# Sixteen gate projections as two-by-two block products, on one core of a Trainium2 chip

## The reference

```python
proj = jnp.einsum('bsd,de->bse', x, w_in[l])            # 1024 x 1024 times 1024 x 5120
ya = _stick_breaking_attention(qa, ka, va)              # 8 heads of 64
yb = _rms_norm(_differential_attention(q1, q2, k1, k2, vb, lam), subln_gain[l])   # 4 heads
gate_a = jax.nn.sigmoid(proj[..., c_vb:c_ga])           # 1024 x 1024
gate_b = jax.nn.sigmoid(proj[..., c_ga:])               # 1024 x 1024
merged = gate_a * einsum(ya, w_branch_a) + gate_b * einsum(yb, w_branch_b)
x = _layer_norm(ALPHA * x + einsum(merged, w_out), ln1_gain, ln1_bias)
h = jnp.square(jax.nn.relu(einsum(x, w_ff1)))
x = _layer_norm(ALPHA * x + einsum(h, w_ff2), ln2_gain, ln2_bias)
```

## Time and profile before

| | us |
|---|---|
| median of three runs (1473.4 to 1474.14) | 1473.87 |
| profiled execution, its own time | 1474.28 |
| span of the profiled execution | 1472.3 |
| PE busy | 1457.4 (99%) |
| DVE busy | 989.4 (67%) |
| ACT busy | 672.4 (46%) |
| POOL busy | 360.1 (24%) |

### The profile page before, as it was taken

One profiled execution on the slowest core, in us unless ns is written; L12 is line 12 of the kernel. 1 busy time (PEld: TensorE's weight loads), 2 busy tenths in 40 slices (PEclk: granted clock), 3 DMA queues, 4 the chain that ended last, 5 costly groups with the idle time before them and its releaser, 6 DMA issues. The chain is left out here.

```text
span 1472.3 us, 19336 instructions
## 1 busy us (share of the span) xinstructions
PE 1457.4 (99%) x7092; PEld 1213.4 (82%) x7092; DVE 989.4 (67%) x1236; ACT 672.4 (46%) x1101; POOL 360.1 (24%) x280
## 2 busy tenths in 40 slices
PE   9999999999999999999999999999999999999997
PEld 8888888887888888888888887888888888888886
DVE  3676776768857566564366788766664577568767
ACT  3455555556557566542032334444443534433343
POOL 2645545455444333312240130000000000000004
PEclk9999999999999999999999999999999999999999
DMA  5211111211101100112442235444443588745563
GB/s 182 58 29 58 58 43 58 71 57 44 58 30 57 30 15 28 41 60 75 168 159 86 86 114 172 158 157 158 158 157 118 210 295 299 278 143 192 192 199 131
DMA packets 111648, 172.40 MB, mean 117 GB/s; under 512 B 6096, under 2 KB 71888, under 8 KB 111440
## 3 DMA queue, kind: packets, MB, share of 16 engines
q1 hardware_dynamic: 111568, 171.33, 34.1%
HBM read 127.27 MB, written 44.04 MB: 116 GB/s over the span
## 5 line engine op out<-in xcount | busy, mean ns | idle before, releaser
L763 PE MATMUL p_proj<-xt_h,w_hi 128*128 128x512 f32 x640 | 254.0, 397 | 1.0 <-DVE xt_l L1590 1.0
L767 PE MATMUL p_proj<-xt_h,w_lo 128*128 128x512 f32 x640 | 252.6, 395 | 0.0
L765 PE MATMUL p_proj<-xt_l,w_hi 128*128 128x512 f32 x640 | 251.2, 392 | 0.0
L2291 POOL TENSOR_TENSOR w_lo<-w_raw,w_hi 128x512 fp32r<-128x512 f32 x96 | 134.7, 1425 | 205.9 <-DVE w_hi L1598 205.4
L2410 POOL TENSOR_TENSOR row_odd<-row_odd,gains 128x1024 f32<-128x1024 f32 x4 | 10.4, 2633 | 578.7 <-ACT row_odd L1562 578.7
L767 PEld LDWEIGHTS p_proj<-xt_h,w_lo 128*128 128x128 f32 x640 | 120.3, 188 | 23.6
L763 PEld LDWEIGHTS p_proj<-xt_h,w_hi 128*128 128x128 f32 x640 | 120.4, 188 | 23.2 <-POOL w_lo L2291 1.0
L765 PEld LDWEIGHTS p_proj<-xt_l,w_hi 128*128 128x128 f32 x640 | 120.5, 188 | 20.6
L1590 DVE TENSOR_TENSOR d_al<-f_a,d_ah 128x1024 fp32r<-128x1024 f32 x56 | 68.5, 1224 | 80.3 <-ACT d_ah L1479 80.3
L1479 ACT ACTIVATE d_ah<-f_a 128x1024 fp32r<-128x1024 f32 x56 | 59.2, 1057 | 134.3 <-PE p_av L1136 54.9
L1328 ACT ACTIVATE a_t<-p_tr 128x384 fp32r<-128x384 f32 (+3 forms) x96 | 47.2, 492 | 123.4 <-PE p_tr L855 123.3
(11 more groups left out here) (292 smaller groups left out, 3520.7 us busy)
## 6 DMA issues: line engine op xcount, KB each, us to landing
f_a<-h_terms SPq DMA_DIRECT2D x56, 512.0 KB, 3.4
w_raw<-w_in SPq DMA_DIRECT2D x40, 512.0 KB, 3.9
h_terms<-c SPq DMA_DIRECT2D x40, 512.0 KB, 3.0
f_b<-w_ff SPq DMA_DIRECT2D x40, 512.0 KB, 4.9
r<-w_ff SPq DMA_DIRECT2D x32, 512.0 KB, 4.0
gate_rows<-gst SPq DMA_DIRECT2D x12, 512.0 KB, 5.0
y<-x SPq DMA_DIRECT2D x8, 512.0 KB, 7.8
wo_raw<-w_out SPq DMA_DIRECT2D x8, 512.0 KB, 8.6
```

Of the source, the lines that this page charges most:

```text
L763: pe.matmul(o, w_hi[n_slot][:, k, :], xt_h[:, k, cols], start=(k == 0), stop=False)
L765: pe.matmul(o, w_hi[n_slot][:, k, :], xt_l[:, k, cols], start=False, stop=False)
L767: mm = pe.matmul(o, w_lo[n_slot][:, k, :], xt_h[:, k, cols], start=False, stop=(k == KT - 1))
L2291: low = pool.tensor_tensor(w_lo[slot][:, ks, :], w_raw[:, ks, :], w_hi[slot][:, ks, :].bitcast(F32), ALU.subtract)
```

## The change

The gate product is taken in pairs: one tile of gate A and one of gate B. The contraction and the tokens are cut in halves, and so is a pair of output tiles. The 2x2 by 2x2 block product is then made from seven products of a quarter (12 matmuls each, 128 channels by 512 tokens by 4 blocks of the contraction) and sums of blocks before and after. A pair takes 7 x 12 matmuls where it took 2 x 48.

- Each stick-breaking group gets five tiles of block products after its three q, k, v tiles (`VTS`): four of a product whose number is `S_PRODUCT[g]`, and one of product 1. A tile holds the products of two pairs (one per half of `p_proj`), so it has 24 matmuls. The groups have 264 filler matmuls each (288 before). Group 7 gets six tiles and the end of the attention two (`LAST_TILES`, 24 matmuls each, products 2 and 4 of a pair added up with what was made before).
- Four products of the seven have sums of token blocks on one side. DVE makes these sums in each stick-breaking group, in three steps for each half, one step in each of the batches 1 to 6, and the low parts in batches 7 and 8 (`x_sums`, `x_sums_low`; each is 128x1024 in and out of SBUF). ACT rounds them after batches 4 and 7 (`sums_rounded`).
- The sums of weight blocks are made on POOL (`weight_sum`, two subtractions of 128x512 each), 16 in all: one in the prologue and five in each of the groups 0 to 2. SP loads their sources (two 512 KB tiles), and stores and reloads the results by `t_rows`.
- ACT rounds the weights in groups 0 to 3 (`split_high`), DVE no longer does so there. ACT copies the products from PSUM to `pst` (ten halves a group; before, six with a sigmoid), and SP stores them.
- In groups 4 to 6 POOL combines the stored products: `gate_parts(i)`, five additions of 128x512 for each of the eight pairs, after batches 1, 5 and 9; SP loads and stores around it. In group 7 and after it DVE adds the last products to the sums (`gate_sum`, `last_sum`), and PE waits for that before it writes the bank again. The sigmoids of all sixteen gates come after the attention, on ACT.
- The outputs of the stick-breaking groups go through HBM (`y_out`, `y_rows`). The two loops over groups are written out on every engine.

```diff
-        total = 48 * tiles
+        halves = [12] * 12 if self.last else [24] * 6 + [12] * (2 * tiles - 6)
+        self.ends = [int(e) for e in np.cumsum(halves)]
+        self.total = self.ends[-1]
...
+            def product_matmuls(n, h, last):
+                o = p_proj[:, h, :]
+                slot = n % 3
+                for k in range(4):
...
+                    pe.matmul(o, w_hi[slot][:, 4 * h + k, :], rows[0], start=(k == 0), stop=False)
+                    pe.matmul(o, w_hi[slot][:, 4 * h + k, :], rows[1], start=False, stop=False)
+                    mm = pe.matmul(o, w_lo[slot][:, 4 * h + k, :], rows[0], start=False, stop=(k == 3))
...
+                def split_high(n):
+                    act.wait_ge(pj_done, n * 2 - 4)
+                    act.wait_ge(wt_in, arrived(n))
+                    act.activation(w_hi[n % 3][:, :, :], w_raw[:, :, :], ACT.Copy).then_inc(wt_hi, 1)
...
+                    if G.sb:
+                        for t in G.tiles_at(k):
+                            split_high(G.tile(t) + 3)
+                        if k in (4, 7):
+                            sums_rounded(k // 7)
...
-                    tile_due = tile_after(G, k)
-                    if G.sb and tile_due is not None:
-                        split_next(tile_due)
+                    if G.sb:
+                        if 1 <= k <= 6:
+                            x_sums(k)
+                        if k in (7, 8):
+                            x_sums_low(k - 7)
...
+            def weight_sum(n):
+                pool.wait_ge(ws_in, 16 * sum((4, 3)[SUM_AT[m] // 4 % 2] for m in SUM_AT if m <= n))
+                for ks in (slice(0, 4), slice(4, 8)):
+                    made = pool.tensor_tensor(w_new[:, ks, :], w_new[:, ks, :], w_sub[:, ks, :], ALU.subtract)
+                made.then_inc(ws_done, 1)
...
+                    if not G.sb and not G.last and k in (1, 5, 9):
+                        i = 3 * (G.g - SB_GROUPS) + (1, 5, 9).index(k)
+                        if i < KT:
+                            gate_parts(i)
```

More of the change, by code:

```diff
@@ L100, with arrived @@
             HIGH_END[_m, _n + 1] = len(HIGH_END) + 1
+FIRST_VT, LAST_VT = 3, 6
+S_PRODUCT = (5, 6, 3, 7)
+PART = {1: 0, 7: 1, 3: 2, 5: 3, 6: 4}
+BRANCH_TILE = 52
+VTS = {}
+for _g in range(SB_GROUPS):
+    for _v in range(4):
+        VTS[8 * _g + 6 + _v] = (S_PRODUCT[_g], _v)
+    VTS[8 * _g + 10] = (1, _g)
+LAST_TILES = {44 + _i: _i for _i in range(8)}
+LOADS_OF = [2 if _n in LAST_TILES or _n in VTS and VTS[_n][0] in (1, 3) else 1 for _n in range(BRANCH_TILE)]
+SUM_ROW = {5: 0, 6: 1, 7: 2}
+SUM_AT = {1: 0, 4: 1, 6: 2, 7: 3, 8: 4, 10: 5, 11: 6, 13: 7, 15: 8, 16: 9, 18: 10, 19: 11, 21: 12, 23: 13, 24: 14, 26: 15}
+def arrived(n):
+    return 16 * (sum(LOADS_OF[:n + 1]) if n < BRANCH_TILE else sum(LOADS_OF) + 2 * (n - BRANCH_TILE + 1))
 class Group:
@@ L156, in halves_at, with tiles_at @@
     def halves_at(self, k):
-        lo = 24 if k == 0 else self.until[k - 1]
-        hi = self.until[k]
-        return [i for i in range(1, 2 * self.tiles) if lo < 24 * (i + 1) <= hi]
+        lo = 0 if k < 0 else 24 if k == 0 else self.until[k - 1]
+        hi = 24 if k < 0 else self.until[k]
+        return [i for i, e in enumerate(self.ends) if lo < e <= hi]
+    def tiles_at(self, k):
+        return [i // 2 for i in self.halves_at(k) if i % 2 and i < 2 * self.tiles - 1]
 class Chain:
@@ new lines, in store_terms, with store_products @@
+            def store_terms(n):
+                if n not in SUM_AT:
+                    return
+                r, v = divmod(SUM_AT[n], 4)
+                sp.wait_ge(ws_done, SUM_AT[n] + 1)
+                sp.dma_start(t_rows[r, v], w_new[:, :, :].rearrange("p k c -> p (k c)")).then_inc(s_t, 16)
+            def store_products(n):
+                if n not in VTS:
+                    return
+                q, v = VTS[n]
+                first = 2 * list(VTS).index(n)
+                G = Group((n - 3) // 8, True, 8, (n - 3) // 8 == SB_GROUPS - 1)
+                for h in range(2):
+                    sp.wait_ge(pj_plain, G.plain((n - 3) % 8, h) + 1)
+                    sp.dma_start(prod_rows[2 * v + h, PART[q]], pst[(first + h) % 3][:, :])                      .then_inc(s_pst[(first + h) % 3], 16)
@@ new lines, in _, with load_gate_b @@
+            load_last(45)
+            store_parts(7)
+            load_last(46)
+            for i in range(4):
+                load_sum(i)
+            load_last(47)
+            load_last(48)
+            load_sum(4)
+            def load_gate_b(i):
+                sp.dma_start(gate_pairs[i][1][:, :], gate_rows[8 + i]).then_inc(gate_in[i], 16)
+            for i in range(3):
+                load_gate_b(i)
+            load_last(49)
+            load_last(50)
+            store_sum(3)
+            load_sum(5)
@@ L820, in fill_to @@
                         done[0] += 1
-                    if n == 48 * G.tiles:
+                    if n == G.total:
                         for _ in fill:
@@ L988, in _ @@
                     n = 2 * h + j
-                    for _ in range(4):
-                        next(next_gate)
+                    for _ in range(3):
+                        next(last_sums)
                     if n == 0:
@@ L1212, in project_done @@
                 def project_done(k):
-                    for i in ([0] if k < 0 else G.halves_at(k)):
+                    for i in ([] if G.last else G.halves_at(k)):
                         t, h = i // 2, i % 2
@@ L1317, in attention @@
                 project_done(-1)
+                if G.sb:
+                    split_high(G.tile(2))
                 scored = []
@@ L1745, in attention @@
                         combine(u)
-                to_sum, tile_due = [], None
+                        if G.last:
+                            gate_sum(0, u)
+                to_sum, tiles_due = [], []
                 if G.is_rope(0):
@@ L1778, in attention @@
                             peaks(u + 2, 1)
[L1779 to L1780 removed]
+                        for t in tiles_due:
+                            split_next(t)
                     if to_sum:
```

581 lines of the change are left out of this document (382 added, 199 removed).

## The result

The changed kernel takes 1577.48 us (median of 4 executions, 1576.23 to 1578.61) against 1473.68 for the kernel before on the same chip: ratio 1.0704, 95% interval 1.0685 to 1.0722. It is 103.8 us slower. The prediction was 1488 with a range up to 1508, so it has the sign and misses the size by 89 us.

What follows compares the result with a forecast made beforehand. PE bounds the kernel before; with the change, DVE bounds batches 0 to 8 of groups 0 to 3. 1474.3 + 7 (these groups) + 6 (groups 4 to 6) + 1 (group 7 and the end) = 1488.3, predicted as 1488 us, range 1464 to 1508.

Steps and rivals of the forecast that it cites:

- ACT [...] I take 0: Groups 0 to 3: `split_high`'s wait for the load moves to ACT, costing 0 to 2 us a group, taken as 0.
- A shorter tile [...] Cost 0: Cycle of `w_raw`, 8.1 us with nothing queued, fits a product tile's 9.6 us with 1.5 us to spare; cost 0.
- third rival: Weight cycle runs late: POOL's weight sums ahead of `w_lo` make it 11 us against 9.6; +14, 1502 us; chance 0.15.
- The granted clock should stay at 1.00.: PE's clock stays at 1.00, as in group 3 before with PE standing for 1.8 us.
- DVE's sums: Batches 0 to 8, groups 0 to 3: eight sums a group, 1.57 us each beside POOL, bound these batches; net +7 us.
- second rival: DVE bounds the batches, POOL neither disturbs it nor costs time itself; sum under 1.4 us; 1469.6 us; chance 0.18.
- PE's saving: Groups 0 to 3: 24 filler matmuls fewer in each, 96 x 0.2265 = 21.7 us, 5.4 a group.
- first rival: DVE's sums are hidden and PE gains all 21.7 us: 1452.6 us; chance 0.10.
- POOL in groups 4 to 6: `gate_parts` after batch 5 delays `k_lo`; PE stands about 2 us a group, +6 us, bounds 0 and 12.
- The fourth rival: POOL's combining holds up groups 4 to 6, 4 us a group instead of 2; 1494 us, up to 1500; chance 0.12.
- Group 7 and the end: PE waits for `gate_sum` on DVE instead of ACT's copy; +1 us, bounds 0 and 6.
- ScalarE's rounding: Groups 0 to 3: eight roundings of 1.06 us a group on ACT lie beside PE; load wait taken as 0.

Runs made afterwards that it cites:

- the reordered kernel: Changed kernel with POOL making `w_lo` first and the weight sum behind it, SP storing a sum after the next weight load: 1537.8 us, 1.0433.
- Another order: Changed kernel with DVE's list in group 7 turned, third tile's weights rounded before the work at the group's start, fourth's one batch later: 1573.08 us, 1.0682.

## Why the prediction was wrong

The sign came out right, though mostly for another reason than the forecast's, and several terms did. The size failed mainly at one place: groups 0 to 3 were to get 7 us longer and got 74.5. Groups 4 to 6 got 13.4 us longer (forecast 6), group 7 and what follows 14.2 (forecast 1).

**The whole sum.** Taken off one after another, the weight sums give 66.8 us (1577.5 to 1510.7), the token sums 20.9 (to 1489.8), combining and group 7 together 17.2 (to 1472.6); what is left is 1.0 under the kernel before. Together that is the 103.8.

**The step that failed: "ACT [...] I take 0" and "A shorter tile [...] Cost 0".** The prediction saw the right queue: `split_high` waits for the load in ACT's list with the copy of `a_t` behind it. It costed the wait from the load of before and took the cycle of `w_raw` as 8.1 us "with nothing queued". In the third rival it added the weight sum as work, 2.85 us, and came to +14. The sum is not only work. It has a wait of its own, for 1 MB that SP issues behind the weight load, and POOL stood 78.2 us in 14 such waits, up to 8.8 us, with `w_lo` ready behind it:

```profile
L2568 POOL TENSOR_TENSOR w_new<-w_new,w_sub 128x512 f32<-128x512 f32 x32 | 54.1, 1710 | 78.2 <-DMA w_sub<-t_rows 49.4 <-DMA w_sub<-w_in 28.8
```

Beside work and source loads, 53 of the 66.8 us are left for the waits, the stores and the second loads, and the reordered kernel, with every sum, load and store kept, gets 39.7 us back. So the third rival named the mechanism and its own test, "an ACT wait for `w_raw` of more than 10 us" (36.2 came), and was given 0.15 and 14 us, about a quarter of those 53. "Against it: PE is two tiles behind" was no cover: the two tiles give PE weights, but what PE lacked was the transposed attention weights, which ACT held up.

**"The granted clock should stay at 1.00."** It was 0.91 to 0.97 in groups 0 to 3, 0.94 in group 7 and 0.976 over the span. The stretch that the prediction read it from had PE standing for 1.8 us in four waits of up to 0.6 us. The Trainium skill (TensorE: Matmul & The Clock Gate, "Part 1: The HAM clock gate") says that the clock follows how busy TensorE has been, at 1.2 GHz after idleness and 2.4 GHz when busy; the trace agrees in the 0.52 behind the stand of 6.3 us. A bound for what it costs here: (1 - 0.976) x 1574.3 = 38 us, of which the part that falls on standing time costs nothing. Without the weight sums the same figure is (1 - 0.991) x 1508.9 = 14 us, with the reordered lists (1 - 0.983) x 1539.0 = 26 us. So the lost clock goes with the waits; what it costs apart from them was not measured.

**DVE's sums: right in price, and near in effect.** The mean of all 32 in the changed kernel is 50.8 / 32 = 1.59 us, the prediction had 1.57. Without the weight sums beside them it is 1.44. Three of the eight forms:

```profile
L1888 DVE TENSOR_TENSOR xs_f<-xs_f,xt_h 128x1024 f32<-128x1024 f32 x6 | 11.3, 1882 | 0.0
...
L1798 DVE TENSOR_TENSOR xs_l<-xs_f,xs_h 128x1024 fp32r<-128x1024 f32 x8 | 11.2, 1402 | 0.0
...
L1890 DVE TENSOR_TENSOR xs_f<-xs_f,xt_h 128x1024 f32<-128x1024 f32 x6 | 9.4, 1562 | 0.0
```

By the lock of the Trainium skill (SBUF — State Buffer, "SBUF: two separate sides") the prediction estimated 1.67, not far off, so these runs don't tell the two apart. Through them the groups were to lose 28.7 us (+7, and the 21.7 saved eaten). The runs show 20.9 without the weight sums and 31.1 beside them. The forecast's own signs also came, once the weight sums were gone: PE's wait for DVE at the transposes is 20.8 us there ("some 25") and 5.8 without the token sums too, and groups 0 to 2 last 93.2 to 93.7 us (95). Group 3 lasts 103.4, not 98.6; why was not traced. The second rival, under 1.4 us a sum, is out.

**PE's saving: not all of it arrives.** Without sums and combining, groups 0 to 3 are 13.8 us shorter than before, though 21.7 are saved and ScalarE's rounding alone, in the kernel before, gives 3.2 more. In these groups PE is busy for 18.1 us less (355.3, before 373.3), and it stands for 4.2 us more (7.7, before 3.5); the granted clock is 1.00 in each of them. Its waits for DVE's subtraction are 6.5 us in the whole kernel, 3.1 before. Why the busy time falls by less than 21.7 us was not traced. The first rival, with all 21.7, is out even with free sums.

**POOL in groups 4 to 6: right in kind, but 13.4 us for the 6 predicted,** and over its high bound of 12. Without the combining the kernel is 15.5 us faster, 14.2 of them in these groups. The prediction found 3.1 to 3.7 us of delay for what stands behind the additions and let the `k_lo` at the group's end be the only one to wait. In group 6 (timeline) all of the list moves:

```profile
665.03 7.54 POOL L2585 TENSOR_TENSOR cmb<-cmb 128x512 f32<-128x512 f32 x5
...
670.28 1.16 DVE L1806 CAST w_hi<-w_raw 128x1024 fp32r<-128x1024 f32 x1 [1.89 <-DMA w_raw<-t_rows]
671.36 1.76 DVE L1915 TENSOR_TENSOR stage<-stage,swap 128x512 f32<-128x512 f32 x1
...
672.54 3.45 POOL L2555 TENSOR_TENSOR w_lo<-w_raw,w_hi 128x512 fp32r<-128x512 f32 x2
...
674.29 1.11 ACT L1473 ACTIVATE om<-p_z,vecs 128x1024 f32<-128x1024 f32 x1 [4.66 <-DVE vecs L1945]
...
676.04 0.55 PE L1039 MATMUL p_tr<-small,be 128*128 128x128 f32 x3 [3.96 <-ACT w_t L1529]
```

Beside POOL's 7.5 us, DVE's rounding of weights takes 1.16 us, where it took 0.69, and its rotary sum (beside the last addition and the `w_lo` behind it) 1.76 where it took 0.77. DVE is late with the maximum of the scores, ACT with its exponential, and PE stands 3.96 us in the middle of the group. The fourth rival, 4 us a group, was the nearer one: against the kernel without the combining, the groups are 4.0, 4.1 and 6.2 us longer.

**Group 7 and the end: +14.2 for +1, and over the bound of 6.** Here too a load stands in the way. DVE stands 6.40 us for a reload with `gate_sum` behind it in its list, and PE 7.12 us for the bank.

```profile
705.17 0.69 DVE L1806 CAST w_hi<-w_raw 128x1024 fp32r<-128x1024 f32 x1 [6.40 <-DMA w_raw<-t_rows]
...
709.59 0.77 PE L938 MATMUL p_proj<-xt_h,w_hi 128*128 128x512 f32 x1 [7.12 <-DVE gst L1868]
```

Another order takes 4.4 us of it away. Two more waits of PE, which the kernel before does not have, lie in the branches, for DVE's low parts of the attention's output (`y_l`). And behind the 7.12 us, PE is granted 0.61 of its clock for 6.6 us:

```profile
PE p_tr L1187 <- DVE y_l L2105: 2.9, 1, 2.9
...
PE p_z L1154 <- DVE y_l L2105: 1.6, 1, 1.6
...
709.60:716.20 6.60, 6.60 (x22) 5.35 (x23) 1.06 (x3) 0.92 (x4) 0.00 (x0) 0.61 0.94 301
```

The stands are 11.6 us, and (1 - 0.61) x 6.6 = 2.6 us of clock are lost behind the first, together the 14.2 by which this part grew. That is read from the trace; why DVE is late in the branches was not tried. Even in the kernel without sums and combining, with that order, the granted clock of group 7's first 77 us is 0.93:

```profile
583.00:660.00 77.00, 70.92 (x371) 60.08 (x371) 47.15 (x77) 25.60 (x76) 19.92 (x15) 0.93 0.41 136
```

This part keeps the change from paying even without its sums: groups 0 to 3 gain 13.8 us, and it, 19.0 us longer in the profiled execution that lay 5.7 us over its median, takes about as much.

**ScalarE's rounding: taken at 0 to +2 us a group, is a gain.** It is worth 3.2 us in the kernel before and some 5.9 in the changed one. DVE, which gave it up, is the tighter engine (67% busy, ACT 46%), but that this is the reason is not shown: in the kernel before, PE's waits for DVE's subtraction fall only from 3.1 to 1.8 us.

## What to carry to other kernels

A new operation that is fed by a transfer is to be costed by where it stands in its engine's list: ask what is behind it that was ready, and follow that through every list to the engine that bounds the kernel. Here 16 such operations with 54 us of work on an engine busy a quarter of the time cost 67 us, and moving them behind the work that others wait for, to where their sources have arrived, gave 40 back. Where two lists hang on one buffer, as `w_raw` here, work out its whole cycle with the waits in it, here 14.4 us at one place where the prediction had 8.1. And set a saving in matmuls against the stands that come with it: the saving here was 22 us, and a single stand of 6.3 us cost some 9, with the half clock behind it. Even where the clock held, only 14 of the 22 us arrived.

## What the runs showed of the hardware

- After PE had stood for 6.3 us in group 1 it was granted 0.52 of its clock for the next 6.2 us, and a matmul of 128x512 started every 0.43 us, not every 0.2265. By half of 6.2 us, some 3 us are lost on top of the stand.
- The sixteen pairs of 512 KB source tiles, 16 MB more through the same queue as the weight loads, cost 1.0 us when nobody waited for them, which is within the spread of the runs.
- DVE's rotary sum of 128x512 took 0.77 us beside a POOL subtraction and 1.76 us in group 6, beside POOL's last addition and the subtraction behind it. What tells the two apart was not tried.
